# Gathering x for four expert visits at once in two f32r parts, with rearranged norms, in a two-layer trunk on one Trainium2 core

## The reference

```python
h = adaln(rmsnorm(yp, g_pre_ffn[li]), m_ctx[3], m_ctx[4])
f = moe_ffn(h, ...)
yp = yp + m_ctx[5] * rmsnorm(f, g_post_ffn[li])

def rmsnorm(x, g):
    return x * rsqrt(mean(x * x) + EPS) * g
def adaln(h, shift, scale):
    return h * (1 + scale) + shift

# moe_ffn, after the choice of experts and gates
hid = silu(einsum('td,edf->tef', t, w_gate)) * einsum('td,edf->tef', t, w_up)
routed = einsum('tef,efd->td', hid * gates, w_down)
```

## Time and profile before

| | |
|---|---|
| median of 3 runs | 1410.64 us (1410.25 to 1410.72) |
| the profiled execution | 1410.46 us, of which the span is 1408.5 us |
| mean granted TensorE clock | 0.977 of 2.4 GHz |
| busy, share of the span | PE 95%, weight loads 50%, DVE 33%, ACT 24%, POOL 5% |
| read from HBM | 494 MB, 353 GB/s over the span |

### The profile page before, as it was taken

The page is one execution under the profiler, slowest core; times in us unless marked ns, Lnnn a source line. Parts: engine busy times, 40 slices in busy tenths (PEclk is TensorE's granted clock), DMA queues, the critical chain, the costliest instruction groups (busy, mean ns, idle before and its releaser), DMA issues.

```text
span 1408.5 us, 27115 instructions
## 1 busy us (share of the span) xinstructions
PE 1340.3 (95%) x10630; PEld 705.1 (50%) x10630; DVE 470.0 (33%) x1120; ACT 335.6 (24%) x596; POOL 66.7 (5%) x91
## 2 busy tenths in 40 slices
PE   4889989999999999999979997999999999999996
PEld 2667744444544444454448774544444444444443
DVE  0536482222222222222256457422222222222223
ACT  1425441111111111111153455111111111111111
POOL 0301020000000000000023002000000000000000
PEclk9999989999999999999989998999999999999999
DMA  9889458999999999999694944699999999999990
GB/s 367 328 337 361 172 242 335 392 420 400 410 411 414 401 413 405 414 402 410 291 341 171 366 174 179 242 394 407 417 403 409 408 406 411 412 404 407 416 401 33
DMA packets 86293, 497.40 MB, mean 353 GB/s; under 512 B 7728, under 2 KB 7728, under 8 KB 36336
## 3 DMA queue, kind: packets, MB, share of 16 engines
q1 hardware_dynamic: 84416, 491.58, 86.8%
q0 software_dynamic: 1840, 5.31, 1.0%
HBM read 494.24 MB, written 2.62 MB: 353 GB/s over the span
## 4 chain that ended last, share of the span: by engine, by line
PE 90%; DVE 3%; DMA 3%; ACT 2%; SPq 1%; issue 1%; POOL 1%; POOLq 0%; ACTq 0%; DVEq 0%
PE PS L886 31%; PE PS L916 16%; PE PS L862 13%; PE PS L686 10%; PE PS L878 9%; DMA weights<-in_w_in 3%; PE PS L827 2%; PE PS L707 1%; PE PS L904 1%; PE PS L851 1%; SPq L390 1%; PE PS L779 1%; PE PS L525 1%; DVE h L1223 1%; PE PS L870 1%
## 5 line engine op out<-in xcount | busy, mean ns | idle before, releaser
L886 PE MATMUL PS<-weights,gathered 128*32 128x512 f32 (+1 forms) x3968 | 451.3, 592 | 0.0
L886 PEld LDWEIGHTS PS<-weights,gathered 128*32 128x32 f32 (+1 forms) x3968 | 133.6, 111 | 306.3 <-issue 306.3
L916 PE MATMUL PS<-weights,hiddenT 128*32 128x512 f32 (+1 forms) x1984 | 233.0, 595 | 0.0
L862 PE MATMUL PS<-pick,x_parts 128*128 128x256 bf16 x1632 | 191.2, 272 | 1.0 <-DVE gathered L1524 1.0
L862 PEld LDWEIGHTS PS<-pick,x_parts 128*128 128x128 bf16 x1632 | 151.9, 96 | 76.2 <-issue 55.8
L1560 DVE SCALAR_TENSOR_TENSOR hidden<-PS,slot_gate,silu 128x256 f32<-128x256 f32 x64 | 31.0, 485 | 393.7 <-ACT silu L1113 393.7
L1120 ACT ACTIVATE y_hi<-PS 128x512 fp32r<-128x512 f32 x128 | 76.4, 597 | 294.3 <-PE PS L916 294.3
L1570 DVE TENSOR_TENSOR y_lo<-PS,y_hi 128x512 fp32r<-128x512 f32 x128 | 88.6, 692 | 139.7 <-ACT y_hi L1120 139.7
L686 PE MATMUL PS<-weights_split,hT_high 128*128 128x512 f32 x448 | 112.9, 407 | 12.2 <-ACT hT_high L971 6.8
L1113 ACT ACTIVATE silu<-PS 128x256 f32<-128x256 f32 x64 | 24.6, 384 | 418.3 <-PE PS L886 418.3
L916 PEld LDWEIGHTS PS<-weights,hiddenT 128*32 128x32 f32 (+1 forms) x1984 | 60.5, 110 | 121.6 <-issue 114.6
(11 more groups left out here) (267 smaller groups left out, 929.8 us busy)
## 6 DMA issues: line engine op xcount, KB each, us to landing
weights<-in_w_gate SPq DMA_DIRECT2D x128, 1024.0 KB, 7.9
weights<-in_w_up SPq DMA_DIRECT2D x128, 1024.0 KB, 11.7
weights<-in_w_down SPq DMA_DIRECT2D x128, 1024.0 KB, 9.3
weights<-in_w_ada SPq DMA_DIRECT2D x24, 2048.0 KB, 13.4
weights<-in_w_in SPq DMA_DIRECT2D x9, 2048.0 KB, 17.3
weights<-in_w_out SPq DMA_DIRECT2D x4, 2048.0 KB, 10.2
weights<-in_w_in SPq DMA_DIRECT2D x2, 1024.0 KB, 23.8
weights<-in_ws_gate SPq DMA_DIRECT2D x2, 1024.0 KB, 4.8
```

Source lines behind the costliest of these rows:

```text
L862: last = mm(PS[:, 5 + k, 2 * jj * P:2 * (jj + 1) * P].rearrange("p (u s) -> p u s", u=2), x3[:, g, part, 4 * half + 2 * k + jj, :], pick[: ...
L886: last = mm(PS[a:z, 4, :].rearrange("p (a n) -> p a n", a=2), xgT[:, b, j, a:z], w[:, e, :, j, :], start=j == 0, stop=j == KT - 1, tile_po ...
L916: last = mm(PS[a:z, bank, :], hidT[:, j, a:z], w[:, e, j, n * HALF:(n + 1) * HALF], start=j == 0, stop=j == FT - 1, tile_position=(0, a), ...
```

## The change

The features are gathered a quarter per visit (2 blocks), for four visits at once, with x in two f32r parts: 2 blocks x 2 groups x 2 parts = 8 products of 512 columns. Blocks alternate between banks 5 (ACT) and 6 (DVE). pick gets four slots and a copy in f32r (pickr). Loops unroll four visits on PE, ACT and DVE; SP's stays at two. The first gathers fill what the first visits need: blocks 0 to 3 for one or two visits before the shared down product, blocks 4 to 7 for three or four visits between its two token groups, after a wait for the table and for the choices of visits 2 and 3. The third part's copies go. The count of visits is rounded up to a multiple of four.

In post_norm the sum is multiplied by the gain first (group 1, then group 0), beside the squares, and one instruction per group follows each root; ACT's squares of group 1 wait for the product of group 1. In pre_norm x times gain comes first for both groups, then the second modulation vector where there is one, then one instruction per group. Some tiles move.

```diff
+AHEAD = 4
-    x3 = sb("x_parts", [P, NG, 3, KT, P], bf16)
-    xgT = sb("gathered", [P, 2, KT, P])
-    pick = sb("pick", [P, 2, NG, P + 6 + P], bf16)
+    x2 = sb("x_parts", [P, NG, 2, KT, P], f32r)
+    xgT = sb("gathered", [P, AHEAD, KT, P], at=h_at)
+    pick = sb("pick", [P, AHEAD, NG, P + 6 + P], bf16)
+    pickr = sb("pick_rows", [P, AHEAD, NG, P], f32r)
...
 # TensorE
-                    pe.wait_ge(S["xg_a"], 1)
-                    pe.wait_ge(S["xg_d"], 1)
-                    gather(1)
                     pe.wait_ge(shT_ready, l + 1)
                     wsd = use_block(pe, l, ("shared_dn",))
                     for g in range(NG):
+                        if g:
+                            pe.wait_ge(S["xg_a"], 1)
+                            pe.wait_ge(S["xg_d"], 1)
+                            pe.wait_ge(S["slots_done"], 1)
+                            pe.wait_ge(table_ready, l + 1)
+                            pe.wait_ge(S["picked"], AHEAD)
+                            for odd, banks in enumerate(((5, 4), (6, 7))):
+                                gather(4 + odd, 3, banks[0], 0)
+                                gather(6 + odd, 4, banks[1], 0).then_inc(S["ga_mm"], 1)
...
-                def gather(half):
-
-                    for k in range(2):
-                        for jj in range(2):
-                            for g in range(NG):
-                                for part in range(3):
-                                    last = mm(PS[:, 5 + k, 2 * jj * P:2 * (jj + 1) * P].rearrange("p (u s) -> p u s", u=2),
-                                              x3[:, g, part, 4 * half + 2 * k + jj, :], pick[:, :, g, 0:P],
-                                              start=(g, part) == (0, 0), stop=(g, part) == (1, 2), skip_group_check=True)
-                        last.then_inc(S["ga_mm"], 1)
+                def gather(j, ahead, bank, at):
+
+                    for g in range(NG):
+                        for part in range(2):
+                            last = mm(PS[:, bank, at:at + ahead * P].rearrange("p (u s) -> p u s", u=ahead), x2[:, g, part, j, :],
+                                      pickr[:, 0:ahead, g, :], start=(g, part) == (0, 0), stop=(g, part) == (1, 1), skip_group_check=True)
+                    return last
...
-                    pe.wait_ge(S["picked"], i + (b + 3))
+                    pe.wait_ge(S["picked"], i + (b + AHEAD + 1))
                     pe.wait_ge(S["ylo_done"], i * 2 + (2 * b + 2))
-                    gather(b)
+                    for odd in range(2):
+                        gather(2 * b + odd, AHEAD, 5 + odd, 0).then_inc(S["ga_mm"], 1)
...
-                pe.wait_ge(S["picked"], 2)
-                gather(0)
+                pe.wait_ge(S["picked"], FIXED)
+                for odd in range(2):
+                    gather(odd, 1, 5 + odd, 0)
+                    gather(2 + odd, 2, 5 + odd, P).then_inc(S["ga_mm"], 1)
...
-                with pe.Fori(FIXED, count, 2) as i:
-                    for b in range(2):
+                with pe.Fori(AHEAD, count, AHEAD) as i:
+                    for b in range(AHEAD):
                         visit(i, b, TILES)
 # ScalarE
-                norm_squares(lambda g: PS[:, 2 * g:2 * g + 2, :].rearrange("p a n -> p (a n)"))
+                sum_squares(4 * l + 3, lambda g: PS[:, 2 * g:2 * g + 2, :].rearrange("p a n -> p (a n)"))
+            def sum_squares(q, src):
+
+                for g in range(NG):
+                    if g:
+                        act.wait_ge(scaled, NG * (q // 2) + 1)
...
 # VectorE
-            def pre_norm(q, bcasts):
-                for g in range(NG):
-                    dve.wait_ge(rstd_ready, NG * q + g + 1)
-                    dve.wait_ge(bcast, bcasts)
-                    step(v.scalar_tensor_tensor(h[:, g, :], x[:, g, :], rstd[:, g:g + 1], mb[:, 1, g, :], ALU.mult, ALU.mult))
-                    settled()
-                    v.tensor_tensor(h[:, g, :], h[:, g, :], mb[:, 0, g, :], ALU.add).then_inc(h_ready, 1)
+            def pre_norm(q, bcasts, between):
+
+                dve.wait_ge(bcast, bcasts)
+                for g in range(NG):
+                    dve.wait_ge(resid, NG * (q // 2 - 1) + g + 1)
+                    step(v.tensor_tensor(mb[:, 1, g, :], x[:, g, :], mb[:, 1, g, :], ALU.mult))
+                between()
+                settled()
+                for g in range(NG):
+                    dve.wait_ge(rstd_ready, NG * q + g + 1)
+                    v.scalar_tensor_tensor(h[:, g, :], mb[:, 1, g, :], rstd[:, g:g + 1], mb[:, 0, g, :], ALU.mult, ALU.add)\
+                        .then_inc(h_ready, 1)
...
+            def post_norm(q, src, bcasts, summed):
+
+                done = NG * (q // 2)
+                dve.wait_ge(bcast, bcasts)
+                dve.wait_ge(*summed)
+                v.tensor_tensor(mb[:, 2, 1, :], src(1), mb[:, 2, 1, :], ALU.mult).then_inc(scaled, 1)
+                dve.wait_ge(squares, NG * q + 1)
+                v.tensor_tensor(mb[:, 2, 0, :], src(0), mb[:, 2, 0, :], ALU.mult).then_inc(scaled, 1)
+                dve.wait_ge(scaled, done + NG)
                 for g in range(NG):
                     dve.wait_ge(rstd_ready, NG * q + g + 1)
...
+                    v.scalar_tensor_tensor(x[:, g, :], mb[:, 2, g, :], rstd[:, g:g + 1], x[:, g, :], ALU.mult, ALU.add).then_inc(resid, 1)
...
-                    v.tensor_tensor(pick[:, u, :, 0:P].rearrange("p g (e s) -> p g e s", e=2), iota, slots, ALU.is_equal)
+                    for rows_ in (pick[:, u, :, 0:P], pickr[:, u, :, :]):
+                        v.tensor_tensor(rows_.rearrange("p g (e s) -> p g e s", e=2), iota, slots, ALU.is_equal)
...
-                        v.tensor_tensor(pick[:, u % 2, :, a:z], C["slot"][:, 0:n].unsqueeze(1).to_broadcast([P, NG, n]),
-                                        RK[:, :, bass.ds(code, 1)].to_broadcast([P, NG, n]), ALU.is_equal)
+                        for rows_ in (pick[:, u % AHEAD, :, a:z], pickr[:, u % AHEAD, :, a:z]):
+                            v.tensor_tensor(rows_, C["slot"][:, 0:n].unsqueeze(1).to_broadcast([P, NG, n]),
+                                            RK[:, :, bass.ds(code, 1)].to_broadcast([P, NG, n]), ALU.is_equal)
...
+                for u in range(FIXED, AHEAD):
+                    choose(u, *codes_of(u))
+                codes = codes_of(AHEAD)
                 dve.wait_ge(S["ga_mm"], 4)
-                gathered(1)
-                choose(FIXED, *codes_of(FIXED))
+                gathered(5, 3, 6, 0)
+                gathered(7, 4, 7, 0).then_inc(S["xg_d"], 1)
+                choose(AHEAD, *codes)
```

More of the change, by code:

```diff
@@ L120, in program @@
     x = sb("x", [P, NG, D])
+    h_at = cursor[0]
     h = sb("h", [P, NG, D])
@@ L927, in _ @@
                 shared_down()
-                for b in range(FIXED):
-                    visit(0, b, FIXED_TILES)
+                for b in range(AHEAD):
+                    visit(0, b, FIXED_TILES if b < FIXED else TILES)
                 pe.wait_ge(table_ready, l + 1)
                 count = pe.value_load(n_visits[0:1, 0:1], min_val=PAIRS, max_val=VISITS)
-                with pe.Fori(FIXED, count, 2) as i:
-                    for b in range(2):
+                with pe.Fori(AHEAD, count, AHEAD) as i:
+                    for b in range(AHEAD):
                         visit(i, b, TILES)
@@ L996, in norm_squares @@
                         act.wait_ge(ready, count + g + 1)
+                    run(h[:, g, :], src(g), ACT.Square, scale=D ** -0.5, accum_out=ss[:, g:g + 1]).then_inc(squares, 1)
+            def sum_squares(q, src):
+                for g in range(NG):
+                    if g:
+                        act.wait_ge(scaled, NG * (q // 2) + 1)
                     run(h[:, g, :], src(g), ACT.Square, scale=D ** -0.5, accum_out=ss[:, g:g + 1]).then_inc(squares, 1)
@@ L1088, in _ @@
                     rows_out(3 * l + 2, (g,))
-                    run(x3[:, g, 0, :, :], h[:, g, :].rearrange("t (p j) -> t j p", j=KT), ACT.Copy).then_inc(x_hi, 1)
-                for g in range(NG):
-                    act.wait_ge(x_rest, NG * l + g + 1)
-                    run(x3[:, g, 1, :, :], h[:, g, :].rearrange("t (p j) -> t j p", j=KT), ACT.Copy).then_inc(x_mid, 1)
+                    run(x2[:, g, 0, :, :], h[:, g, :].rearrange("t (p j) -> t j p", j=KT), ACT.Copy).then_inc(x_hi, 1)
                 act.wait_ge(rlog_mm, l + 1)
@@ L1097, in _, with gathered @@
                     run(ssilu[:, g, :], PS[:, 2 + g, 0:F], ACT.Sigmoid).then_inc(sh_silu, 1)
-                def gathered(half):
-                    return xgT[:, :, 4 * half:4 * half + 2, :].rearrange("p u j s -> p j u s"), \
-                        PS[:, 5, :].rearrange("p (j u s) -> p j u s", j=2, u=2)
+                def gathered(j, ahead, bank, at):
+                    return run(xgT[:, 0:ahead, j, :], PS[:, bank, at:at + ahead * P].rearrange("p (u s) -> p u s", u=ahead), ACT.Copy)
```

(25 more changed lines are left out.)

72 lines of the change are left out of this document (34 added, 38 removed).

## The result

The changed kernel takes **1363.8 us** (median of 4 runs, 1363.3 to 1364.6); the kernel before took 1410.7 beside it. The ratio is 0.9670, 95% interval 0.9658 to 0.9683: 46.9 us or 3.3% faster. Timed again with five runs it took 1365.7 us (1365.3 to 1368.8; ratio 0.9687, interval 0.9674 to 0.9701).

A forecast was written before the change was run, and what follows sets the result against it. PE was taken to bound the expert loops. Per layer -19.2 (gather) + 1.5 (transfers) + 3.7 (stage start) - 0.9 - 1.1 (norms) = -16.0; two layers -32.0, from 1410.46 to 1378.5 us, range 1369 to 1393.

The forecast's parts named there:

- the wait for the choices: Start of each expert stage: PE stands still 1.8 us before the second initial gather until choices 2 and 3 come.
- the second gather: Start of each expert stage: 16 products, 8 of 384 and 8 of 512 columns, at 0.20 each, take 3.6 us.
- the start of the stage: From scores to visit 0 in each layer: visit 0 begins 3.7 us later, ends +1.9 and +5.0.
- The one-hots, the evacuations and the split copies: Expert stage: DVE's added one-hots and the evacuations cost nothing in the visit; the first copies in two pieces add a little.
- The code rival: Expert loop: the doubled body no longer stays in place; four blocks refetched in each of 14 passes add 50 us: 1429; chance 0.05.
- The f32r rival: Gather in the expert loop: f32r runs like f32, 8 products take 3.5 us, about 1481 in all; chance 0.02.
- The gather, 0.60 per visit: Expert loop: 8 f32r products replace 24 bf16 ones and save 0.60 us per visit (0.55 to 0.65), 19.2 per layer.
- The transfers, +1.5 per layer: Expert loop: PE waits for expert weights 1.5 us per layer, ends 0 and +6.
- the tie: Expert loop: PE needs 451.8 us while 186.6 MB of weights take 449.6 us at 415 GB/s.
- the transfer rival: Expert loop: transfers bound early at a sustained 409 GB/s, the wait is 6 us per layer: 1387.5; chance 0.18.
- The norms: Norms with the gain product beside the squares: -0.9 us per layer after the mixer, -1.1 after the experts, each 0 to -1.9.
- first row of PE waiting for expert weights: Sign that the forecast is right: PE's waits name expert weights for the first time, a few us in all.

The follow-up runs named there:

- the run with less scatter: The changed kernel with the low part of y left out of the scatter (4 of 8 products per visit): 1361.6 us, ratio 0.9643.
- the later gather: The changed kernel with the second initial gather behind 12, not 8, of the 16 shared down products: 1364.6 us (0.9660), timed again 1365.7 us (0.9686).

## Why the prediction was wrong

**What held.** PE bounds and goes on bounding; in layer 0 the wait for the choices (1.93 for 1.8), the second gather (3.34 for 3.6) and the start of the stage as a whole (+3.6 for +3.7) came as worked out. In layer 1 the start is near by luck (+4.3): a lower clock took the place of the wait. The one-hots, the evacuations and the split copies stayed hidden, as said. The code rival fell: the page counts 32 blocks, not the 80 that a refetch of four in each of 14 passes needs, and PE has no idle time in the windows of the loops. That agrees with what the forecast drew from the Trainium skill's "Runtime: NRT & Kernel Launch" (Instruction fetch mechanics). The f32r rival fell with the first row of L869. The mechanism was right, and three terms of the sum were mis-sized.

**The gather, 0.60 per visit: 0.70.** The step "the scatter is the same kind and number: 1.97 us ... the out-projection ... 1.95 for 8" compared two different lengths. The 2.54 us of the old gather ran from its first load to the next group's first load. So measured, eight products of 512 columns take 1.75 us, not 1.95: the next load runs beside the last product, whose columns the 1.95 counts. The scatter's 1.97 holds a wait of its load path that the gather has not (0.27). Of the 0.79 us that this makes, the two transposes behind the gather take 0.11 back (0.34 us of load path for 0.23), and the scatter gives 0.02: 0.70. Over 64 visits (45.1 / 64 = 0.70) that is 6.7 us of the miss, and 0.70 lay outside the ends of 0.55 and 0.65 too.

**The transfers, +1.5 per layer: 0.** The step "at 415 GB/s (the middle between 409, which the loop moves while PE paces it, and 423, its best stretch)" averaged a demand with a ceiling. 409 was PE's pace; the run with less scatter showed 422 sustained with PE waiting. The time that came of it was right by luck: in layer 0 the 186.6 MB took 448.2 us (230.35 to 678.57), or 416 GB/s, for the 449.6 of the sum. At 422 they would take 442; about half of the other 6 us is the loop's start, which the sum left out (380 GB/s over the first 30 us). What failed is the step from the tie to +1.5: "Stretches at 388 leave debts that the shrinking lead no longer covers". These stretches are gone once more blocks are under way: all 40 slices of 10 us of the changed loop from 270 to 670 us lie between 416 and 424. PE needed 448.7 us for the same stretch, so it was a tie indeed, and the 0.5 us of lead at visit 31 kept the wait at 0. This is 3.0 us of the miss, and the transfer rival at 0.18 with its 1387.5 took 409 for a rate. Of the two figures of the Trainium skill, the 408.7 GB/s in "DMA: Bandwidth & Descriptors" (iDMA fabric) lies below the 422 measured here, which decides, and the 425 or so in "HBM Reference" (Specifications) is near it. By the latter the forecast would have been 1375.5.

**The router product, not in the sum: -3.8 us in the first profile, -2.1 in the second.** Its 5.55 us were taken as fixed, though they were run half at the lower clock. With the new norms PE's transposes before it stand in one group, and the clock's fall can then end before the product starts, as it did in the first profile; that the grouping is the cause is argued, not shown. Over all profiles of this study the product took 3.64 us in none of 6 cases with the old norms, in 7 of 12 with new norms and two parts. Within a program it is chance, not a fixed gain, and how much of these 2 to 4 us a run gets is luck.

**The norms: -5.1 for -4.0**, inside the stated ends. But the step "this frees time beside the router product and nothing on the path" (the third part of x) was wrong in what it left out: that freed time is the condition for the norms' gain. With the third part in place the norms gave 0.4 us (0.9997); with it gone, 5.6 to 7.5.

Of the forecast's signs, "first row of PE waiting for expert weights" did not come, though the lead shrank to almost nothing by visit 31 as forecast: the loop takes 14.70 us per visit, its transfers 14.91.

## What to carry to other kernels

A bandwidth read from a loop that another engine paces is a demand, not a ceiling: look for the stretches in which several blocks are under way throughout, take the best of them as the rate, and count the transfers' start as a term of its own. Measure what a group of instructions holds of an engine between the same two edges on both sides of a comparison, best from load to load. And when one change moves work in time, ask which other part of it clears the place the work moves to: here each of the norms, the width and the later gather was worth nothing by itself.

## What was not expected of the hardware

- Narrow f32r products cost little more per column than wide ones: 8 of 512 columns hold the weight path for 1.75 us and 16 of 256 columns for 1.89, though each 128x128 f32r load lasts 0.188 us (0.096 for bf16). In the narrow form the loads follow each other every 0.12 us, so they overlap one another, and their length does not set the pace.
- The transfers sustain 422 GB/s for hundreds of microseconds with blocks of 1024 KB, three or more of them under way at any time, whether or not PE waits.
- The granted clock between mixer and experts falls at a moment that differs from one execution to the next of the same program: at 181 us in one, at about 187 in the other. The same 16 router products take 3.64 us in one and 5.33 in the other (up to 6.5 in other kernels here), and the two profiled spans differ by 1.9 us.
